# Two layers of sequence mixers in one kernel: the last layer's mixers restaged, and the forgetting attention's value products turned round

## The reference, cut to what matters

```
s = einsum("bthd,bshd->bhts", qb, k) * scale + fb[..., :, None] - big_f[..., None, :]
s = where(k_pos <= q_pos, s, -inf);  p = softmax(s)
out = einsum("bhts,bshd->bthd", p, v)
```

```
dots = einsum('bqhd,bsd->bqhs', iqb, ik) * idx_scale
score = einsum('bqh,bqhs->bqs', iwb * w_scale, relu(dots));  score = where(admissible, score, -inf)
_, sel = top_k(score, 256)
p = softmax(where(valid, einsum('bqhr,bqkr->bqhk', ql, c_sel) * scale + bias, -inf))
```

## Time and profile before

| | |
|---|---|
| median of 3 runs | 5283.35 us (5280.79 to 5286.9) |
| the profiled execution | 5289.84 us |
| its span in the trace | 5288.2 us, mean granted TensorE clock 0.827 |

### The profile page before, as it was taken

The page is one execution under the profiler, slowest core; times in us unless marked ns, Lnnn a source line. Parts: engine busy times, 40 slices in busy tenths (PEclk is TensorE's granted clock), DMA queues, the critical chain, the costliest instruction groups (busy, mean ns, idle before and its releaser), DMA issues. The chain is left out here.

```text
span 5288.2 us, 65270 instructions
## 1 busy us (share of the span) xinstructions
PE 4384.3 (83%) x23498; PEld 3313.7 (63%) x23498; DVE 2679.4 (51%) x5418; ACT 1921.6 (36%) x3904; POOL 712.9 (13%) x745
## 2 busy tenths in 40 slices
PE   7997899983578888898899999956688887876679
PEld 6876777772466666676787888833344444544567
DVE  3114444454555544544212111138988888887546
ACT  3112232333323323333102010113677767777621
POOL 3111111100000000000000000012223333434400
PEclk9998999985677767767899999976577887878779
DMA  5337666653000000000423212120000001011033
GB/s 181 117 120 240 206 219 216 200 183 129 28 23 24 23 23 23 23 12 5 166 96 115 82 68 76 55 61 23 18 19 19 19 19 37 19 37 37 24 126 116
DMA packets 203971, 426.38 MB, mean 81 GB/s; under 512 B 37544, under 2 KB 67916, under 8 KB 203484
## 3 DMA queue, kind: packets, MB, share of 16 engines
q1 hardware_dynamic: 203648, 422.20, 23.2%
HBM read 300.47 MB, written 121.65 MB: 80 GB/s over the span
## 5 line engine op out<-in xcount | busy, mean ns | idle before, releaser
L3162 POOL TENSOR_TENSOR ds_E<-ds_bT 128x256 f32<-128x256 f32 x112 | 72.9, 651 | 2869.0 <-ACT ds_bT L3131 2683.6
L2651 PE MATMUL ds_big<-ds_ikT,ds_iqT 64*128 64x512 f32 (+3 forms) x640 | 378.0, 740 | 90.2 <-ACT ds_iqT L2628 56.5
L301 PE MATMUL g_acc<-g_ws_hi,g_hT_hi 128*128 128x512 f32 (+1 forms) x1024 | 386.9, 378 | 0.0
L303 PE MATMUL g_acc<-g_ws_hi,g_hT_lo 128*128 128x512 f32 (+1 forms) x1024 | 385.3, 376 | 0.0
L302 PE MATMUL g_acc<-g_ws_lo,g_hT_hi 128*128 128x512 f32 (+1 forms) x1024 | 385.2, 376 | 0.0
L2714 DVE TENSOR_SCALAR_CACHE_REDUCE ds_eq<-ds_hi,ds_num 128x2048 uint16<-128x2048 uint16 (+13 forms) x224 | 331.3, 1479 | 25.7 <-issue 3.5
L529 PE MATMUL mm_big<-mm_gw_hi,mm_ghT_hi 128*128 128x512 f32 (+1 forms) x768 | 318.5, 415 | 30.4 <-PEq L134 30.4
L530 PE MATMUL mm_big<-mm_gw_lo,mm_ghT_hi 128*128 128x512 f32 (+1 forms) x768 | 300.2, 391 | 0.0
L531 PE MATMUL mm_big<-mm_gw_hi,mm_ghT_lo 128*128 128x512 f32 (+1 forms) x768 | 300.2, 391 | 0.0
L2754 ACT ACTIVATE ds_signs<-ds_lo,ds_at 128x2048 bf16<-128x2048 uint16 (+13 forms) x224 | 291.3, 1300 | 1.2
L328 DVE COPY g_stage<-g_acc 128x512 f32<-128x512 f32 (+1 forms) x64 | 41.5, 649 | 459.2 <-PE g_acc L303 459.2
(11 more groups left out here) (512 smaller groups left out, 10307.8 us busy)
## 6 DMA issues: line engine op xcount, KB each, us to landing
mm_ghT_hi<-turned SPq DMA_DIRECT2D x96, 512.0 KB, 4.1
mm_ghT_lo<-turned SPq DMA_DIRECT2D x96, 512.0 KB, 5.4
proj<-g_stage SPq DMA_DIRECT2D x112, 256.0 KB, 2.0
proj<-mm_gstage SPq DMA_DIRECT2D x80, 256.0 KB, 5.0
mm_x<-proj SPq DMA_DIRECT2D x64, 256.0 KB, 3.9
second_raw<-in_w_in SPq DMA_DIRECT2D x56, 256.0 KB, 4.1
proj<-fp_stage SPq DMA_DIRECT2D x48, 256.0 KB, 2.0
mm_graw<-in_w_in SPq DMA_DIRECT2D x40, 256.0 KB, 6.5
```

Source lines behind the costliest of these rows:

```text
L301: pe.matmul(sums, hT.hi[:, k, tile], wt.hi[:, k, 0:width], start=(k == 0), stop=False)
L303: mm = pe.matmul(sums, hT.lo[:, k, tile], wt.hi[:, k, 0:width], start=False, stop=(k == KD - 1))
L2651: pe.matmul(big[:, n % 2, 0:wd], iqT[o, h // 2], b.ikT[o, x:x + wd], start=True, stop=True)\
```

## The change: what it does

Four edits to the last layer and one to the first.

1. **Order of tiles.** `PLAIN` = 2 tiles (0 and 1) get no `index_scores` and no `upper_half`. Index scores run for tiles 15 to 2 in steps 0 to 13. The tiles to be attended are 1, 0, 15, 14, ..., 2: `lower_half` of the k-th of them in step k, `attend` in step k+1. So tiles 1 and 0 are attended in steps 1 and 2, tiles 15 to 5 in steps 3 to 13 as before, and tile 2 in step 16. The steps become 18; the last holds one store.
2. **Bias.** Load and mirroring both stand in step 0.
3. **One setup step** in place of six. The keys' turning starts before the norm, half of it on either side of the bias table; ScalarE keeps the turned keys; the HGRN's bounds are worked out among the rest; temporary tensors lie in the score, selection and logit buffers.
4. **Last weights.** In step 16 `last_weights` loads and splits `w_o`, beside the attention of tile 2, into buffers that `project_out` then takes (`held`). With `held` that phase loads no weights, and `columns(2)` waits for the turning of tile 0 alone.
5. **Forgetting attention, tiles 4 to 15** (`folded`). In `weigh` the values are the weights in the array (128 by 64) and the probabilities are streamed (128 by 128). Even key blocks write partitions 0 to 63 of bank 7, odd ones partitions 64 to 127, as channel by query. After the last block ScalarE copies the sums (128 by 512), and four matmuls with `fold` (identity of 64 twice, one above the other) add both halves and turn them back.

```
@@ fox_attend
+    sums = big[:, 7].rearrange("p (h t) -> p h t", h=HEADS)
+    folded = k >= FOLDED
+    if folded:
+        uses.append((("o",), None))
     turns = in_turn([5, 6], uses)
+    o = big[:, turns["o",][0] if folded else 7, 0:GW].rearrange("p (h d) -> p h d", h=HEADS)
 (scalar, at the end)
+        if folded:
+            yield 11 / N
+            act.wait_ge(s.f_weighed, HEADS * NP)
+            act.activation(pT[:, 0], sums, ACT.Copy).then_inc(s.f_sums_kept, 1)
 (vector, at place 11 / N)
-        dve.wait_ge(s.f_weighed, HEADS * NP)
+        if folded:
+            dve.wait_ge(s.f_folded, 1)
+        else:
+            dve.wait_ge(s.f_weighed, HEADS * NP)
 (tensor, at the end)
+        if folded:
+            yield 11 / N
+            take(pe, "o")
+            pe.wait_ge(s.f_sums_kept, 1)
+            for h in range(HEADS):
+                m = pe.matmul(o[:, h], pT[:, 0, h], b.fold[:], start=True, stop=True)
+            m.then_inc(s.f_folded, 1)
 (weigh)
+            at = x // P + t
+            v, w = b.v[:, at, h * HD:(h + 1) * HD], pT[:, (h * NP + p) % 2, t]
+            if folded:
+                m = pe.matmul(sums[(LOW, HIGH)[at % 2], h], v, w, start=(at < 2), stop=(at + 2 > k))
+            else:
+                m = pe.matmul(o[:, h], w, v, start=(at == 0), stop=(at == k))
@@ project_out
+                if held:
+                    columns(1)
+                else:
                     (the loop over w_out, with columns(1) in it)
                     sp.wait_ge(s.w_lo, K)
                 rows(0)
                 rows(1)
                 columns(2)
@@ bias_flip (now with the load; tensor at 0.4 + 0.12 h, vector at 0.45 + 0.12 h)
@@ last_mixers_setup (new), one step
+        sync:   ik (2 DMAs), ct, g, rb, onehot, lb (2), hg, iw, iq, q, f, uk, uv; wait bias_kept; table; wait all
+        vector: memset state; memset at; [c_in] sq = ct*ct; reduce; [g_in] ct*g; [rs] ct*ss; [biases] copy table;
+                [lb_in] max; 2 subtractions; [turned] copy cT; [expd] add; reciprocal; mult; 2 scalings; scale hg
+        scalar: [squares] rstd; [ik_t 1] copy half of ikT; [ik_t 2] copy the other half; [diffd] Exp of lb
+        tensor: [ik_in] 8 transposes of ik; [oh_in] 5 matmuls for the biases; [bias_kept] 8 transposes of ik;
+                [ik_kept 2, normed] 16 transposes of ct
@@ last_weights (new)
+    def sync(sp):
+        for k in range(D_MODEL // P):
+            yield 0.01 * k
+            if k >= 3:
+                sp.wait_ge(s.pw_lo, k - 2)
+            sp.dma_start(b.x[:, k % 3], w_out[k * P:(k + 1) * P, :]).then_inc(...)
+    scalar at 0.1 + 0.11 k: wait for the DMA, high part (ACT Copy) of piece k
+    vector at 0.15 + 0.11 k: wait for the high part, low part (subtract) of piece k
@@ second_mixers
+    order = list(range(TILES - 1, PLAIN - 1, -1))
+    attended = list(range(PLAIN - 1, -1, -1)) + order
+    N = len(order)
-        for k in range(TILES + 4):
+        for k in range(TILES + 2):
+                if k == 0:
+                    branches.append(bias_flip(c, bias, s, big, table))
+                if k < N:
+                    branches.append(index_scores(c, ib, s, proj, big, order[k]))
+                if 1 <= k <= N:
+                    branches.append(upper_half(c, tb, s, order[k - 1]))
+                if k < TILES:
+                    branches.append(lower_half(c, tb, s, attended[k]))
+                if 1 <= k <= TILES:
+                    after = attended[k] if k < TILES else None
+                    branches.append(attend(c, ab, s, proj, big, attended[k - 1], after))
+                if k < TILES:
+                    branches.append(hgrn_chunk(c, hb, s, proj, k))
+                if k == TILES:
+                    branches.append(last_weights(last, s, w['w_o_2']))
```

More of the change, by code:

```diff
@@ L1083, in fox_rwkv_and_gating @@
             ub = sgu_buffers(nc, c, E, w)
-            with step(nc, "sgu_in gains_in ahead_in turned masked scaled cleared") as (block, s):
+            with step(nc, "sgu_in gains_in ahead_in turned masked scaled cleared folds") as (block, s):
                 @block.sync
@@ L1105, in _ @@
                     dve.memset(carry[:], 0.0).then_inc(s.cleared, 1)
+                    dve.tensor_tensor(fb.fold[:], c.ident[:, LOW], c.ident[:, HIGH], ALU.add).then_inc(s.folds, 1)
                     dve.wait_ge(s.gains_in, 48)
@@ L1321, in weigh @@
         for t in range(wd // P):
-            m = pe.matmul(o[:, h], pT[:, (h * NP + p) % 2, t], b.v[:, x // P + t, h * HD:(h + 1) * HD],
-                          start=(p == 0 and t == 0), stop=(x + (t + 1) * P == W))
+            at = x // P + t
[4 more added lines that the diff above has]
+                m = pe.matmul(o[:, h], w, v, start=(at == 0), stop=(at == k))
         m.then_inc(s.f_weighed, 1)
@@ L2458, in _ @@
                 keep(0)
-                for k in range(K):
+                if held:
+                    keep(1)
+                for k in range(0 if held else K):
                     act.wait_ge(w_in[k % 3], 16 * (k // 3 + 1))
@@ L2481, in _ @@
                 rest(0)
-                for k in range(K):
+                if held:
+                    rest(1)
+                for k in range(0 if held else K):
                     dve.wait_ge(s.w_hi, k + 1)
@@ L2526, with bias_flip @@
 BIAS_SIGNALS = "bias_in flipped flip_kept "
-def bias_load(bias, s, table):
+def bias_flip(c, bias, s, big, table):
     def sync(sp):
@@ L2670, in threshold_buffers @@
     return b
-def threshold_setup(nc, b):
-    with step(nc, "start_set") as (block, s):
-        @block.vector
-        def _(dve):
-            dve.memset(b.at[:, 2:3], -32767.5).then_inc(s.start_set, 1)
 SELECT_SIGNALS = "low_found "
@@ L2827, in attend_loads, with attend @@
     return 16
-def attend(c, b, s, proj, big, k):
+def attend(c, b, s, proj, big, k, after):
     H, R = 4, P
@@ L2871, in sync @@
         sp.dma_start(gate[:].rearrange("p h d -> p (h d)"), proj[tok, E_G:E_G + H * P]).then_inc(s.g_in, 16)
-        if k:
-            n = attend_loads(b, sp, s.q_ahead, proj, k - 1)
+        if after is not None:
+            n = attend_loads(b, sp, s.q_ahead, proj, after)
             yield 1.0
@@ L3301, in second_mixers @@
+LAST_SIGNALS = "pw_in0 pw_in1 pw_in2 pw_hi pw_lo "
+def second_mixers(nc, c, w, proj, mix, table, onehot, x_old, out):
     H, R, KEEP = 4, 128, float(TOPK)
+    order = list(range(TILES - 1, PLAIN - 1, -1))
+    attended = list(range(PLAIN - 1, -1, -1)) + order
+    N = len(order)
     with ExitStack() as ctx:
@@ L3390, in second_mixers @@
-        order = list(range(TILES - 1, -1, -1))
-        for k in range(TILES + 4):
+        banks, early = ctx.enter_context(ExitStack()), ctx.enter_context(ExitStack())
+        big = Buffers(nc, banks, "ds").ps("big", [P, 8, 512])
+        E = Buffers(nc, early, "ds")
+        ikT, score = E.sb("ikT", [P, SEQ]), E.sb("score", [P, 3, SEQ])
+        ib = index_buffers(E, ikT, score)
+        tb = threshold_buffers(E, score, sel)
+        hb = hgrn_buffers(E, big, y)
+        last_mixers_setup(nc, c, w, proj, table, onehot, ib, tb, ab, hb)
@@ L3421, in _ @@
                     stores = 0
-                    if k >= 4:
-                        t = order[k - 4]
+                    if k >= 2:
+                        t = attended[k - 2]
                         sp.dma_start(mix[t * P:(t + 1) * P, 0:512], ab.q[:, t % 2]).then_inc(s.stored, 16)
@@ L3450, in _ @@
                     together(pe, "tensor", branches)
+        banks.close()
+        project_out(nc, c, mix, w['w_o_2'], x_old, out, "pf", ln=(w['ln_g_2'], w['ln_b_2']), held=last)
 def program(nc, t, consts, onehot, out):
```

285 lines of the change are left out of this document (147 added, 138 removed).

## The result

The changed kernel took 5237.14 us (5234.19 to 5238.8, 4 runs) against 5285.12 us (5280.79 to 5290.55, 4 runs) on the same chip: a ratio of 0.991, 95% interval 0.9894 to 0.9926, so 48 us less. That is inside the forecast's range and near the slow end of the range of its main case (5190 to 5245), with 48 us gained where 70 were forecast. The profiled execution took 5238.8 us, 51.0 less than the one before, with the same mean granted clock (0.827).

What follows compares the result with a forecast made beforehand. TensorE's list was taken to bound forgetting-attention steps 4 to 15; VectorE, chains and setup filled last-layer steps. Last layer -60 and forgetting attention -10 gave -70: 5220 us profiled, 5214 median, range 5172 to 5275 (main case 5190 to 5245, chance 0.60).

Steps and rivals of the forecast that it cites:

- Steps 17 and 18: Last layer: both steps go, as tiles 1 and 0 are attended earlier, -38.6 us.
- The filling: Last layer, steps 1 and 2: attending tiles 1 and 0 there adds VectorE work paid at 1.2 for 1, +9 us.
- rival C: Steps 1 and 2 cost +30 over the 9, step 16 +20 over the 6: total -20, 5263 us; chance 0.10.
- Step 16: Last layer: loading and splitting the last weights beside tile 2's attention makes 32 us against 25.7, +6.
- The last projection: Without its eight weight pieces, TensorE's idle time before tile 2's turning, slow restart and late first products go, -13 us.
- A: Forgetting attention: the array's halves take turns, so +51 in place of -10, total -9, 5274 us; chance 0.12.
- B: Forgetting attention: halves take turns and each weight load is exposed, +114, total +54, 5337 us; chance 0.04.
- The setup: Last layer: one setup step, a chain starting when `ct` lands at +10.3, takes 37.6 us against 58.7, -21.
- Steps 14 and 15: Last layer: without index scores VectorE has less work, though neither step is VectorE's; -3.5 and -1.5 us.
- TensorE -37: Forgetting attention, tiles 4 to 15: overlapping halves gain 71, shape changes cost 28; 0.85 of the remaining 43 us reaches the end.
- the tail: Forgetting attention, each step's end: the division waits for the fold, delaying VectorE's last copy 2.1 us or more, +27 in all.
- Rival D: Forgetting attention: more columns streamed in half the time raise the clock, in step 14 and others, -30 more, 5184 us; chance 0.14.

Runs made afterwards that it cites:

- 7: The changed kernel with tiles attended in the old order (15 to 2, then 1, 0) in twenty steps, tiles 1 and 0 still unscored: 5265.74 us.
- 4: The changed kernel with all key blocks of the value products in one half of the array, so no pairs: 5216.82 us.
- 5: The changed kernel with no tile folded, value products streaming 128 columns instead of 64 under the same weights, division in two operations: 5206.57 us.
- Kernel 11: The changed kernel unfolded with 128 streamed columns, the setup reordered, and the last weights issued ahead of the wait for the store: 5185.18 us.
- 8: The changed kernel with HGRN chunks 14 and 15 left out, their outputs not computed: 5204.31 us, one run.
- 10: The changed kernel with the last weights loaded and split in the last projection again, as before the change: 5238.73 us.
- e1_unfolded: The changed kernel with every tile of the forgetting attention in the old, unfolded form: 5251.24 us.

## Why the prediction was right, and where it was wrong

**Right.** The sign, the rough size, and six of nine windows within 3 us, because each was read between barriers. Steps 17 and 18 went whole. The filling cost 11.4 (forecast 9) at VectorE's rate (rival C said 39), and 7 shows it alone: 12.8. Step 16 came to 32.5 (forecast 32), with VectorE waiting 14.7 us for ScalarE's high parts. The last projection lost the idle gap ahead of tile 2 as said. Rivals A and B are refuted by 4: the column halves overlap. The sentence of the Trainium skill behind B (TensorE: Matmul & The Clock Gate, What overlaps and what doesn't) lets a weight load overlap a running matmul only where their row groups differ; all blocks here share their rows, and pairs still took 0.59 us for eight records against 1.02. In 5, 64 more columns streamed by each record added only 0.06 us to eight records, so full-row matmuls run beside full-row loads too. The Trainium skill's other sentence (TensorEngine Tiling (Array Packing), Key Properties), that tiles run in parallel, is what this trace shows.

**Wrong: last layer, 44 in place of 60.**

- *The setup, -17 in place of -21.* The step that failed is "`ct` lands 10.3 after the start": it was 12.8 (3457.0 to 3469.82), as its issue began 3.0 after the start and its landing took 9.8 more, not 7.8. (Two issues of 1.5 and 7.8 to landing are 10.8 even by the prediction's own figures.) Behind it, the bias matmuls could only start when the one-hot table landed (3471.67), 1.9 after the first VectorE instruction instead of beside it. They took the same 8.69 us at the lower clock as before, so the table's copy ended 13.4 after that instruction, not 11.9. The rest of the chain took 15.6, forecast 15.4. Kernel 11 shows that the order was worth 6 to 8 us more.
- *Steps 14 and 15, -0.9 in place of -5.* What failed is that the clock was left where it was. At equal low time the removed scores are worth 3.5 and about 1 us (see 8), as forecast; the two steps had 24 us more of low time than before (75.1 against 51.2), and that took it back.
- *Steps 3 to 13, +5.6 in place of 0.* They were left at their times. The drift is mostly step 7 (+5.7), and it is the clock's: the eleven steps have 16.6 us more of low time (446.5 against 429.9), 12.6 of it in step 7. Why it falls there is not shown.
- *Filling, +2.4*, as above.

The early weights were forecast well as windows (+6 and -13) and still mis-credited: 10 shows that without them tile 2's step took 19.0, not 25.7, since its clock came up. Without them the two windows fell by 7.7 (250.4 to 242.7), with them by 7.1, so the -7 was the clock's and not theirs.

**Right for a wrong reason: the forgetting attention, -8.9 against -10.** "TensorE -37" failed in the 0.85. TensorE's own side was near: `weigh` fell by 50.6 us (forecast 71 less 28, that is 43), and the fold's matmuls, which the forecast had in the tail only, (1.1 x 12) took back 13 of it; 5 I could not place. The tail was sized well (2.0 us a step, +23 to +27). What failed is the assumption behind both, that the clock stays where it was and a us of TensorE's list is worth 0.85 of the time. At an equal clock the fold is worth nothing (697, 700), where 10 us were forecast; the measured gain goes with 40 us less of low time than in `e1_unfolded`, or 29 less than before. That 8.9 came so near to 10 is luck. Rival D had the right quantity. Its event came (step 14, -23.2), but it came also in the old kernel when that ran again (91.1), so most of it was chance, and the other steps gave back 14.3. And D's reasoning, more columns in half the time bring the clock up, is contradicted by 4: the form with pairs has 100 us more of low time than the one without, whose TensorE list is 43 us longer in that line.

What is shown: low time in this stage goes with the form of `weigh` (490 to 521 us in the old one, 480 with pairs, 380 in one half, 355 to 389 with more streamed columns) and costs 0.3 to 0.4 us a us. The differences of 100 us and more are clear of the scatter within a form, that between the old form and pairs is not. What is not shown: why these forms have these low times. Each experiment changes the streamed columns, the load's width or the overlap together with the gaps between records, and none separates them.

## What to carry to other kernels

Cut the trace at the barriers, name for each stretch the chain that ends it, and credit removed work only if it is on that chain. Before TensorE's list is shortened, work out the time at the lower clock in that stretch and its price from two executions of the same code; a form with fewer us of TensorE work can lose more in granted clock than it saves, and a wider operand under an unchanged weight load can cost little and come with a higher clock. Compare a window only with one of like low time before you credit or blame an edit for it: two of the drifts here were the clock's. Undo each edit alone, the ones that met their forecast too: one here was worth under 2 us although both of its windows came as said.

## What the runs showed that was not expected

- Streaming 128 columns in place of 64 under a 128-column float32 weight load cost TensorE 0.06 us for eight records at full clock (0.90 against 0.84), and came with 145 us less of low time in the stage.
- Two column halves that share their rows overlap (0.59 against 1.02 us for eight records), and the kernel that does without it is faster.
- The lower clock level can fill 93.9 of a step's 105.9 us in one execution and 57.0 of 91.1 in the next (step 14 of the same kernel), while the ten steps ahead of it repeat to 0.1 us.
